# Identity matmuls into an unread PSUM bank during norms, and prompt attention's stages one unit further apart

## What is computed

```
# layer 0: even_mixer (retention and spatial gating), layer 1: nsa (sparse attention)
for l in range(DEPTH):
    hp = rms_norm(xp, norm_mix_pre[l]); hs = rms_norm(xs, norm_mix_pre[l])
    mp, ms = mixer(hp, hs)
    xp = xp + rms_norm(mp, norm_mix_post[l]); xs = xs + rms_norm(ms, norm_mix_post[l])
    fp, fs = conv_ffn(rms_norm(xp, norm_ffn_pre[l])), conv_ffn(rms_norm(xs, norm_ffn_pre[l]))
    xp = xp + rms_norm(fp, norm_ffn_post[l]); xs = xs + rms_norm(fs, norm_ffn_post[l])

def rms_norm(x, g):
    return x * lax.rsqrt(jnp.mean(x * x, -1, keepdims=True) + EPS) * g
```

## Time and profile before

| | |
|---|---|
| three executions | 1702.52, 1702.55, 1703.31 us (median 1702.55) |
| profiled execution | 1702.67 us, its span 1701.0 |
| PE busy | 1586.1 us (93%), weight loads 1449.9 (85%) |
| DVE, ACT, POOL busy | 785.4 (46%), 686.7 (40%), 219.7 (13%) |
| granted TensorE clock, mean | 0.968 of 2.4 GHz |
| DMA | 138.46 MB, mean 81 GB/s |
| attention, first scores to last value product | about 943 to 1129 us |

### The profile page before, as it was taken

How to read it: one execution, slowest core, us unless ns; L and a number is a source line. 1 busy time by engine, 2 the same in 40 slices (tenths; PEclk the granted TensorE clock), 3 DMA queues, 4 the chain that set the end, 5 groups by cost and what they waited for, 6 DMA issues and landing times.

```text
span 1701.0 us, 31079 instructions
## 1 busy us (share of the span) xinstructions
PE 1586.1 (93%) x12951; PEld 1449.9 (85%) x12951; DVE 785.4 (46%) x1274; ACT 686.7 (40%) x1312; POOL 219.7 (13%) x582
## 2 busy tenths in 40 slices
PE   5999989899999999979999899987969999999996
PEld 4999978699999999969999555554959999999995
DVE  4555462555532555344112566642165552255523
ACT  3122134355532555223322565654335552355422
POOL 3000001200000000001013344431100000000000
PEclk8999999999999999988999899999979999999998
DMA  6212317122233332323234300013311323323231
GB/s 214 88 64 75 100 62 187 42 74 76 82 92 91 88 86 71 95 74 101 82 101 88 149 1 2 1 53 98 86 50 50 98 60 106 99 76 93 60 88 53
DMA packets 185559, 138.46 MB, mean 81 GB/s; under 512 B 11376, under 2 KB 177504, under 8 KB 185392
## 3 DMA queue, kind: packets, MB, share of 16 engines
q1 hardware_dynamic: 175536, 106.31, 22.0%
q0 software_dynamic: 9920, 30.74, 5.8%
HBM read 128.21 MB, written 13.01 MB: 83 GB/s over the span
## 4 chain that ended last, share of the span: by engine, by line
PE 68%; DVE 5%; ACT 3%; issue 3%; POOLq 2%; POOL 1%; DMA 0%; DVEq 0%; ACTq 0%
PE gemm L897 40%; PE gemm L590 9%; PE gemm L601 8%; PE misc L565 4%; PE gemm L1035 1%; PE misc L1066 1%; POOLq L498 1%; ACT pr L1210 1%; DVE pr L1890 1%; DVE y L1606 1%; PE gemm L638 1%; DVE xT L1610 1%; PE misc L659 1%; ACT pT_rows L1210 1%; POOL pr L2168 1%
## 5 line engine op out<-in xcount | busy, mean ns | idle before, releaser
L1572 DVE TENSOR_TENSOR wL<-raw,wH 128x2048 fp32r<-128x2048 f32 (+2 forms) x107 | 222.1, 2075 | 239.1 <-ACT wH L1210 239.1
L897 PE MATMUL gemm<-hH,wH 128*128 128x272 f32 x1280 | 268.5, 291 | 0.1
L897 PE MATMUL gemm<-hH,wL 128*128 128x272 f32 x1280 | 264.9, 288 | 0.0
L897 PE MATMUL gemm<-hL,wH 128*128 128x272 f32 x1280 | 264.0, 288 | 0.0
L1210 ACT ACTIVATE wH<-raw 128x2048 fp32r<-128x2048 f32 (+2 forms) x107 | 185.2, 1731 | 52.9 <-PE gemm L590 32.7
L897 PEld LDWEIGHTS gemm<-hH,wH 128*128 128x128 f32 x1280 | 200.5, 188 | 6.2 <-issue 4.9
L897 PEld LDWEIGHTS gemm<-hL,wH 128*128 128x128 f32 x1280 | 201.1, 188 | 0.0
L897 PEld LDWEIGHTS gemm<-hH,wL 128*128 128x128 f32 x1280 | 199.9, 189 | 0.0
L1810 DVE SCALAR_TENSOR_TENSOR conv<-up,rows_t,conv 128x560 f32<-128x560 f32 x88 | 70.6, 802 | 213.0 <-ACT conv L1210 213.0
L601 PE MATMUL gemm<-wH,hH 128*128 128x256 f32 x544 | 156.4, 288 | 9.5 <-DVE hL L1583 5.5
L601 PE MATMUL gemm<-wL,hH 128*128 128x256 f32 x544 | 156.1, 287 | 0.0
(11 more groups left out here) (345 smaller groups left out, 2704.6 us busy)
## 6 DMA issues: line engine op xcount, KB each, us to landing
raw<-in_f_w_in SPq DMA_DIRECT2D x88, 512.0 KB, 4.8
raw<-in_f_w_out SPq DMA_DIRECT2D x32, 704.0 KB, 4.6
raw<-in_e_w_in SPq DMA_DIRECT2D x12, 1024.0 KB, 5.1
raw<-in_o_w_in SPq DMA_DIRECT2D x10, 1024.0 KB, 5.3
raw<-in_e_w_out SPq DMA_DIRECT2D x4, 1024.0 KB, 5.6
pages<-in_cache_cmp POOLq DMA_DIRECT2D x16, 256.0 KB, 3.6
raw<-in_o_w_out SPq DMA_DIRECT2D x16, 256.0 KB, 5.6
rows<-in_cache_sel POOLq DMA_DIRECT2D x12, 256.0 KB, 2.9
```

Of the source, the lines that this page charges most:

```text
L897: ins = pe.matmul(gemm[odd][:, n, 0:TH], w, x[:, k, n * TH:(n + 1) * TH], start=(k == 0 and part == 0), stop=(k == nk - 1 and part == 2))
L1572: order(dve.tensor_tensor(unit_view(wL, u), unit_view(raw, u), unit_view(wH, u).bitcast(F32), ALU.subtract), lo_ready)
```

## The change

It has two parts. On PE, `stay_busy(count)` multiplies the identity by itself `count` times into the first 128 columns of `b7`, from which nobody reads the result. It is called at the start, behind a semaphore of its own for the identity's load (14 times), around norm 0's spread (6 and 12), before the spread of norms 3, 5 and 7 (6), in norms 4 and 6 (`next_norm`: 12 ahead, 3 after each of seven sums, 6 after the eighth, 10 after the spread), and before the wait for the last rotated queries ahead of attention (8). In `ffn`, PE also waits for the last tail copy out of `b7`. In prompt attention, `LAG` goes from 3 to 4, `turn_probs` stands ahead of `scores` on PE, `take_probs` stands first in the loops of ACT and DVE, `exps` is one iteration later on ACT and `normalise` one later on DVE. POOL's loop is unchanged.

```diff
-        N_UNITS, LAG = 72, 3
+        N_UNITS, LAG = 72, 4
...
-            sp.dma_start(ident[:, :], a["ident"]).then_inc(x_in, 16)
+            sp.dma_start(ident[:, :], a["ident"]).then_inc(ident_in, 16)
...
+            def next_norm(n, sq):
+                stay_busy(12)
+                for m in range(DC):
+                    square_sum(n, m, sq)
+                    stay_busy(3 if m < DC - 1 else 6)
+                spread_rstd(n)
+                stay_busy(10)
...
-            pe.wait_ge(x_in, 64)
+            def stay_busy(count):
+                for _ in range(count):
+                    pe.matmul(b7[:, 0:P], ident[:, :], ident[:, :], start=True, stop=True)
+
+            pe.wait_ge(ident_in, 16)
+            stay_busy(14)
+            pe.wait_ge(x_in, 48)
...
             square_sum(0, DC - 1, sqx)
+            stay_busy(6)
             spread_rstd(0)
+            stay_busy(12)
...
                 if fill:
                     compress(0, 0, 2)
+                else:
+                    stay_busy(6)
                 spread_rstd(n)
...
                 square_sum(n, DC - 1, sqf)
+                pe.wait_ge(tail_ev, 4 * FH + 1 if layer else 2 * FH + 1)
+                stay_busy(6)
                 spread_rstd(n)
...
-            for m in range(DC):
-                square_sum(4, m, sqf)
-            spread_rstd(4)
+            next_norm(4, sqf)
...
+            stay_busy(8)
             pe.wait_ge(o_ropes, 7)
...
             for n in range(N_UNITS + LAG + 1):
+                if LAG <= n < N_UNITS + LAG:
+                    turn_probs(n - LAG)
                 if n < N_UNITS:
...
                     turn_in(5 + n)
-                if LAG <= n < N_UNITS + LAG:
-                    turn_probs(n - LAG)
...
-            for m in range(DC):
-                square_sum(6, m, sqm)
-            spread_rstd(6)
+            next_norm(6, sqm)
...
             for n in range(N_UNITS + LAG + 2):
-                if n < N_UNITS:
-                    exps(n)
+                if LAG <= n < N_UNITS + LAG:
+                    take_probs(n - LAG)
+                if 1 <= n <= N_UNITS:
+                    exps(n - 1)
                 if 1 <= n < 7 and n % 2:
                     take_in(5 + n)
-                if LAG <= n < N_UNITS + LAG:
-                    take_probs(n - LAG)
...
             for n in range(N_UNITS + LAG + 2):
+                if LAG <= n < N_UNITS + LAG:
+                    take_probs(n - LAG)
                 if n < N_UNITS:
                     mask(n)
...
-                if 1 <= n < N_UNITS + 1:
-                    normalise(n - 1)
-                if LAG <= n < N_UNITS + LAG:
-                    take_probs(n - LAG)
+                if 2 <= n < N_UNITS + 2:
+                    normalise(n - 2)
```

More of the change, by code:

```diff
@@ L356, in build_program @@
         loads, x_in = sem("first_loads"), sem("x_in")
+        ident_in = sem("ident_in")
         consts = sem("consts_set")
```

## The result

The change takes 1686.61 us (median of four executions, 1683.25 to 1689.61) where the kernel before takes 1702.69 (1702.52 to 1703.31): ratio 0.990, 95% interval 0.988 to 0.992, so 16 us less. The profiled execution took 1687.76 us, with a span of 1685.9. The forecast was 1682.4 in 1673 to 1693.

A forecast was written before the change was run, and what follows sets the result against it. TensorE carries 68% of the span, so gains lie in its idle or slow-clock time. Start 1.0, norms 2.1, 4.2 and 3.5, entry 1.0 and attention 8.5 sum to 20.3 us off 1702.7: 1682.4 us, range 1673 to 1693.

The forecast's parts named there:

- Norm 0: End of norm 0: fillers let the products at 32.01 start at the full clock, 2.1 us less.
- norms 5 and 6: Double norm: two spreads faster by 0.94 and 0.98, slow products by 1.6, together 3.5 us less.
- rival 4: Norms and entry: fillers don't hold the clock and PE becomes the norm's bound, slower at 1722 us, chance 0.03.
- Norms 3 and 4: Double norm: with the clock kept up, last sum, spread and products get shorter, together 4.2 us less.
- the last sum is 0.24 shorter: Norm 4: the last sum of squares gains 0.24 us if the clock stays up.
- The spread's 0.98: Norms 3 and 4: the spread takes 1.20 us in place of 2.18, so 0.98 less.
- Start: Kernel start: fillers raise the clock for the first transposes, 1.0 us less, bounds 0 to some 2.5.
- Entry: Into attention: eight fillers speed the turns behind them, and ACT takes a tile earlier; 1.0 us less, bounds 0 to 3.
- Attention: Prompt attention: waits for probability copies go, 13.3 us gained, 4.8 of new POOL waits added; 8.5 us less.
- The signs of being wrong: Clock 0.50 over a filled stretch, sums over 0.1 us after their square, or PE's POOL wait in attention above 8 us.
- rivals 1 and 3: 1: attention's POOL path costs as much as the copies did, 1691, chance 0.17; 3: clock falls in a double norm, 1686, 0.13.
- Rival 2: Attention gives all 13.3 us as waits overlap, entry and start give their upper bounds: 1674 us, chance 0.18.

The follow-up runs named there:

- fillers_alone: The kernel before plus all the identity matmuls, with attention left as before (lag 3, old order): 1691.99 us, ratio 0.9932.
- attention_alone: The kernel before plus only the attention part (lag 4, new order), no identity matmuls anywhere: 1695.59 us, ratio 0.9958.
- change_again: The changed kernel, unedited, timed again in a later set: 1686.02 us, ratio 0.9894 against the kernel before.
- copies_first: The kernel before with only take_probs moved to the front of ACT's and DVE's iteration, lag 3, no fillers: 1703.08 us, ratio 0.9995.
- lag4_alone: The kernel before with LAG 4 in place of 3 and no other edit: 1765.19 us, ratio 1.0353.
- fillers_turn: The change with every filler made of two transposes of the identity in place of one matmul: 1687.34 us, ratio 0.9874.
- fillers_doubled: The change with six fillers in place of three after each of seven sums in norms 4 and 6: 1695.86 us, ratio 0.9934.

## Why the prediction was right, and where it wasn't

The forecast of 1682.4 was 4.2 us too low, and the forecast's mechanism held in both halves: fillers_alone gave 12.0 us for a forecast of 11.8, attention_alone 8.4 for 8.5. That the first came so near is in part luck: in its trace start, norms and entry come to 9.4 us, and another 1.8 were gained in stretches that it doesn't touch. Term by term:

- **Norm 0, norms 5 and 6**: nearly as forecast, 1.9 for 2.1 and 3.4 for 3.5, in every trace with fillers there to within 0.1 us for norm 0. Spreads are 1.19 us, the products start at the full clock, and the identity matmul holds it: rival 4's assumption that it might not is refuted.
- **Norms 3 and 4**: 3.1 for 4.2. The term that failed is "the last sum is 0.24 shorter". I had read that squares come each 1.33 us from the first two sums and applied it to the last, which comes 0.65 behind the seventh. Three fillers made it late: the root starts 2.03 us later in after than before, in a stretch that was 1.67 later as a whole, so 0.36 lost in place of 0.24 gained. The spread's 0.98 came as forecast, less some 0.16. The products gave 2.7 for 3.0, and norm 0 its 1.9 for 2.1, for one reason: I had halved their slow time, but they aren't twice as fast at the full clock. From start to start a product of 256 columns takes 0.21 us at the lower level and 0.12 at the full one, as before's timeline shows around the rise of the clock at 36.3 (below). The 28 products behind norm 4 took 6.1 us slow and 3.4 fast.

```profile
32.36 0.41 PE L601 MATMUL gemm<-wL,hH 128*128 128x256 f32 x1
32.57 0.41 PE L601 MATMUL gemm<-wH,hL 128*128 128x256 f32 x1
...
36.60 0.28 PE L601 MATMUL gemm<-wL,hH 128*128 128x256 f32 x1
36.72 0.28 PE L601 MATMUL gemm<-wH,hL 128*128 128x256 f32 x1
```

- **Start**: 1.0 was forecast within 0 to 2.5. The traces give some 0.6 on average and either sign in one execution. The turns behind the fillers stay at 0.50 in after and at 0.57 in change_again from 11.2 to 19.2. By the Trainium skill's rule on transposes, which I had set beside it, the term was 0; after's trace has no gain either, but not by that rule: its clock fell at 10.3, before the first turn, while PE had no work. What I had wrong is that the 2 us between the fillers and the rows, named in the working, cost the clock.
- **Entry**: 0.4 for 1.0. The clock was up for the turns, which are paced by copies, and fell behind them, among attention's first units (0.74 over 937 to 955).
- **Attention**: 9.4 for 8.5. Of the 14.2 us of waits 1.4 stayed with the copies, 0.9 forecast, and POOL's became 3.6, where I had added 4.8 of new ones. They stand where a group begins, 1.4 us at each second-tile group; of the 1.6 that pairs of units in the smallest tile were to lose, hardly anything came (no wait for POOL above 0.14 us in the second half's). "These waits go" was right, though for half of the reason: I had put it down to the order and the lag together, and copies_first shows that the copy's place alone does it. And that `mask(n)` waits for `turn_probs(n - 4)`, which stood in the description, never entered a rival: lag4_alone lost 60 us by it, and the reordering that comes with the lag keeps the change from that.
- **Not in the forecast**: the long slow head of attention, worth 7.1 us (45.0 - 37.9) in an execution that has it, and the clock and page waits in untouched code. The four executions of the change spread over 6.4 us, with the lowest mean clock (0.977) in the slowest and the highest (0.984) in the fastest. How much of the median's 4.2 us above the forecast is owed to this can't be told from the one that was traced. In the set of change_again the change's halves gave 12.0 and 8.4, 20.4 together, which is the forecast's 20.3; the whole gave 17.9, and the interval (0.9874 to 0.9915, 14 to 21 us) doesn't tell the two apart.
- **The signs of being wrong**: two of the three came. The last sum of norm 4 starts 0.65 us after its square is done (766.36 against 765.71), and the clock stood at 0.50 behind the start's fillers. PE's wait for POOL stayed under 8 us.

Nothing of rivals 1 and 3 was seen: POOL's waits did not grow to what the copies' had been, and no trace with fillers has a fall in the two double norms. Rival 2 had the right sign for attention at the full clock.

## What to carry to other kernels

A filler costs nothing only while it ends before the work behind it may start, and that has to be checked for each gap by itself: the last of a series can come at half the others' distance. When stages of a software pipeline are moved apart, go round each buffer's circle first (who frees the slot, and where that stands in its engine's order); one more unit of lag with four slots made the kernel 60 us slower by itself, of which a part may be the clock's. And where a kernel's executions spread, compare mean granted clocks and cut the trace at fixed landmarks before a difference of a few microseconds is given to an edit.

## What was not expected of the hardware

- A PE that is 99% busy can stay at 1.2 GHz. In change_again it was busy for 27.61 of 28 us at 0.51, with scores over 64 rows, transposes and value products over 64 columns; the slow head lasted 34.1 us there, in fillers_turn and in fillers_doubled, and 10.2 in after, whose instructions are the same. The same kinds of work then run on at the full clock for 140 us without a fall. What decides when the clock comes back there is open; in the four traces with full matmuls of the identity in the middle it was back sooner (3.4 to 6.8 us slow; but fillers_alone, with the old order and none there, had 6.8 too).
- Full-size transposes hold the clock and bring it back: 28 of them at the start of fillers_turn, and the turns of the output in eight traces, as told with that run.
- The clock also fell behind work of few columns without idle time: in change_again it was low from 158.9 to 162.3 with PE busy all the time, behind these 16 records of 4 columns. Ten of the fourteen traces have such a fall between 158 and 185 us, within 1 us of the start of the last of 16 like them and with no idle time ahead of it; the four others have none.

```profile
156.58 1.95 PE L756 MATMUL misc<-qds,s 128*128 128x4 f32 x16
```

- With the clock up, the groups of attention in the change's order repeat from trace to trace within 0.05 us (21.17 to 21.19, 26.11 to 26.12, 17.73 to 17.74). What differs between two traces of the change lies in stretches where the clock or a wait for DMA differs.
